# A decoder layer on one core: two chunks of the next expert's first product moved ahead of the turning of activations, and a weight ring of 16 slots

## The reference

```python
logits = (xf @ w_router + b_router)            # 32 experts, top 4 of them
top_v, top_i = lax.top_k(logits, TOP_K)
gates = jax.nn.softmax(top_v, axis=-1)
...
h = xb @ w1[e] + b1[e]                         # w1: 1024 x 2048 for each expert
x_glu = jnp.minimum(h[:, 0::2], SWIGLU_LIMIT)
x_lin = jnp.clip(h[:, 1::2], -SWIGLU_LIMIT, SWIGLU_LIMIT)
a = x_glu * jax.nn.sigmoid(SWIGLU_ALPHA * x_glu) * (x_lin + 1.0)
y = a @ w2[e] + b2[e]                          # w2: 1024 x 1024
return y.astype(F32) * gate[:, None]
```

## Time and profile before

| | |
|---|---|
| median of three runs | 1804.74 us (1802.44 to 1806.01) |
| profiled execution | 1805.31 us, its span 1803.5 us |
| experts (first token turn to last second product) | 628.9 to 1766.9 us |
| PE busy | 1512.5 us, 84% of the span |
| DMA in the expert stage, as mean busy share of the 16 DMA engines | 0.87 to 0.99 by round |
| TensorE clock granted over the span | 0.88 of full |

### The profile page before, as it was taken

The page is one execution under the profiler, slowest core; times in us unless marked ns, Lnnn a source line. Parts: engine busy times, 40 slices in busy tenths (PEclk is TensorE's granted clock), DMA queues, the critical chain, the costliest instruction groups (busy, mean ns, idle before and its releaser), DMA issues.

```text
span 1803.5 us, 33945 instructions
## 1 busy us (share of the span) xinstructions
PE 1512.5 (84%) x13484; PEld 733.8 (41%) x13484; DVE 432.2 (24%) x1005; ACT 217.2 (12%) x521; POOL 343.7 (19%) x344
## 2 busy tenths in 40 slices
PE   5999977777764599889989989989889989998991
PEld 4775565565431233433324323333333333342330
DVE  1020057332324431221212113112212212122125
ACT  1010020122101010111101011111111111011110
POOL 6120022000012312112112212212132131211212
PEclk9999975555877599999999989999989999999996
DMA  8443110200003479999998998998998999999993
GB/s 252 83 73 93 61 51 6 71 0 1 24 12 120 164 259 374 406 399 339 405 409 305 398 409 313 403 401 302 411 396 309 405 400 343 400 405 371 336 371 108
DMA packets 127719, 468.45 MB, mean 260 GB/s; under 512 B 31862, under 2 KB 52442, under 8 KB 94768
## 3 DMA queue, kind: packets, MB, share of 16 engines
q1 hardware_dynamic: 99088, 425.46, 59.6%
q0 software_dynamic: 27728, 37.99, 9.4%
q10 hardware_dynamic: 736, 2.65, 0.4%
HBM read 443.54 MB, written 23.42 MB: 259 GB/s over the span
## 4 chain that ended last, share of the span: by engine, by line
PE 53%; DVE 9%; issue 3%; DMA 1%; ACT 0%; POOL 0%; SPq 0%; DVEq 0%; POOLq 0%; ACTq 0%
PE PS L1156 32%; PE PS L1179 19%; DVE mix L1598 2%; DVE qmT L1603 2%; DVE qmT L1605 2%; PE PS L1169 1%; DVE qmT L1602 1%; DVE qmT L1599 1%; PE PS L1133 1%; DVE smalls L1646 0%; DVE ring L1656 0%; DVE ring L1658 0%; DMA smalls<-token_lists 0%; DMA expert_rows<-mix,smalls 0%; DMA ring<-expert_rows 0%
## 5 line engine op out<-in xcount | busy, mean ns | idle before, releaser
L1156 PE MATMUL PS<-ring,mix 128*32 128x512 f32 x5632 | 631.5, 603 | 38.5 <-issue 37.1
L1156 PEld LDWEIGHTS PS<-ring,mix 128*32 128x32 f32 x5632 | 190.7, 112 | 461.2 <-issue 449.3
L1179 PE MATMUL PS<-ring,mix 128*32 128x256 f32 x5632 | 345.6, 406 | 0.0
L673 POOL DMA_INDIRECT expert_rows<-mix,smalls x88 | 139.0, 1579 | 886.4 <-issue 657.7
L1179 PEld LDWEIGHTS PS<-ring,mix 128*32 128x32 f32 x5632 | 187.1, 117 | 141.9 <-issue 40.9
L1598 DVE TENSOR_TENSOR mix<-PS,kn 128x512 f32<-128x512 f32 x88 | 60.9, 692 | 564.1 <-PE PS L1156 556.0
L817 ACT ACTIVATE qmT<-qmT 128x256 f32<-128x256 f32 x88 | 36.6, 416 | 665.5 <-DVE qmT L1599 665.5
L911 PE MATMUL PS<-xT,ring 128*128 128x48 f32 (+1 forms) x384 | 104.0, 434 | 0.0
L664 POOL DMA_INDIRECT mix<-x_rows,smalls x94 | 92.8, 988 | 43.4 <-issue 33.4
L1169 PE MATMUL PS<-cst,qmT 128*128 128x128 f32 x176 | 39.5, 308 | 68.5 <-DVE qmT L1605 67.7
L897 PE MATMUL PS<-ring,xT 128*128 128x256 f32 (+1 forms) x400 | 89.7, 386 | 0.6 <-DVE xT L1251 0.6
(11 more groups left out here) (361 smaller groups left out, 968.5 us busy)
## 6 DMA issues: line engine op xcount, KB each, us to landing
ring<-in_w_moe_dram SPq DMA_DIRECT2D x384, 1024.0 KB, 14.5
ring<-in_w_in_dram SPq DMA_DIRECT2D x9, 1024.0 KB, 16.3
ring<-in_w_out_dram SPq DMA_DIRECT2D x4, 1024.0 KB
expert_rows<-X ACTq DMA_DIRECT2D x5, 512.0 KB
X<-in_x_prompt_dram SPq DMA_DIRECT2D x4, 512.0 KB, 5.5
ring<-in_state_mlstm_C_dram POOLq DMA_DIRECT2D x1, 2048.0 KB, 14.8
ring<-in_w_in_dram SPq DMA_DIRECT2D x8, 256.0 KB, 9.8
out_dram<-ring POOLq DMA_DIRECT2D x1, 2048.0 KB, 10.8
```

Source lines behind the costliest of these rows:

```text
L673: nc.gpsimd.indirect_dma_start(out=y_blocks, out_offset=bass.IndirectOffsetOnAxis(ap=lists[a][:, g, 1:2].bitcast(U32), axis=0), in_=ysb[g] ...
L1156: ins = mm(bank(g)[32 * t:32 * t + 32, :], xgT[XBUF[a][g]][:, P * (k % 2) + 32 * (k // 2):P * (k % 2) + 32 * (k // 2) + 32], ring[:, SLOT[ ...
L1179: ins = mm(bank(g)[32 * t:32 * t + 32, 0:256], aT[g % 2][:, P * (f % 2) + 32 * (f // 2):P * (f % 2) + 32 * (f // 2) + 32], rowpair(s)[:, f ...
```

## The change

- **Ring.** Slots 12 and 13 lie over the dead `xT` buffer, 14 and 15 over the dead `X` buffer. Loads go round the 16 slots in the order in which PE uses the chunks; item s waits for item s-16 (`slot_freed`). Bias and lists are loaded after w1's last chunk, a list three experts ahead.
- **PE.** Expert n's chunks 0 and 1 of w1 are multiplied between the first product and the turning of activations of expert n-1. What is left of the first product (chunks 2 to 7) has the turning of the next expert's tokens after chunk 4 instead of after chunk 7. Odd experts accumulate in banks 4 and 5, and activations turn through banks 6 and 7.
- **Loops.** The last round is written out after a loop of seven rounds on every engine. The gathers for experts 32 and 33, whose rows nobody used, are gone.
- Smaller: the router's scratch moves out of `xT`; seven semaphores of the decode attention become two.

```diff
-AHEAD = E + 2
+AHEAD = E
+BANK0 = (0, 4, 0, 4)
+TURN = 4
+EARLY = 2
-SLOT = [3, 4, 5, 0, 1, 2, 6, 7, 8, 9, 10, 11]
+SLOT = [3, 4, 5, 0, 1, 2, 6, 7, 12, 13, 8, 9, 10, 11, 14, 15]
+SLOTS = len(SLOT)
...
+def stream_w1(n, k):
+    return 12 * n + (k - 4 if k < EARLY else k) if n else k
+def stream_w2(n, c):
+    return 12 * n + 8 + EARLY + c
...
+            def slot_freed(j, s):
+                t = s - SLOTS
...
+                b, u = (t - 8) // 12, (t - 8) % 12
+                if u == EARLY + 3:
+                    sp.wait_ge(l2_mm, first_group(j, b + 1))
+                elif u == 11:
+                    sp.wait_ge(l1_mm, first_group(j, b + 2))
+                elif u < EARLY + 3:
+                    sp.wait_ge(chunk_used, j * (10 * ROUND) + (10 * b + 8 + u))
+                else:
+                    sp.wait_ge(chunk_used, j * (10 * ROUND) + (10 * b + 7 + u))
...
+            def expert_loads(j, a):
...
+                    for k in range(EARLY):
+                        s = 12 * a + 8 + k
+                        slot_freed(j, s)
+                        load_chunk(after, k, SLOT[s % SLOTS])
+                for c in range(4):
+                    s = stream_w2(a, c)
...
+                    slot_freed(j, s)
+                    load_chunk(e, 8 + c, SLOT[s % SLOTS])
...
+                for k in range(EARLY, 8):
+                    s = 12 * (a + 1) + k
+                    if isinstance(n, int) and n == 0 and s == 14:
+                        sp.wait_ge(y_set, 16 * (NT + 2))
+                    slot_freed(j, s)
+                    load_chunk(after, k, SLOT[s % SLOTS])
...
+                sp.wait_ge(b1_shuf, n + 1)
+                load_bias(after)
+                if not (isinstance(n, int) and n + 3 >= E):
+                    sp.wait_ge(y_done, first_group(j, a) + 2)
+                    load_list(expert_at(n + 3), (a + 3) % ROUND, a + 3)
...
+            def expert_rows(j, a):
+                n = j * ROUND + a
+                for g in range(GROUPS[a]):
+                    if g == GROUPS[a] - 1 and not (isinstance(n, int) and n + 2 >= E):
+                        gather(n + 2, first_pair(j, a + 1), (a + 2) % ROUND)
+                    scatter(first_group(j, a), a, g, [scattered_before(j, a, b) for b in range(4)])
...
             def expert(j, a):
                 group = first_group(j, a)
+                if not (isinstance(j, int) and j * ROUND + a == E - 1):
+                    turned_tokens(first_pair(j, a + 1), (a + 1) % ROUND)
                 sigmoid(group, 0)
-                turned_tokens(first_pair(j, a + 1), (a + 1) % ROUND)
...
             def expert(j, a):
-                n, group = j * ROUND + a, first_group(j, a)
-                nxt = (a + 1) % ROUND
-                before = GROUPS[a - 1]
-                first_product(n, a, first_pair(j, a + 1), [group + (3 - before + min(g, before - 1)) for g in range(GROUPS[a])])
-                turn_tokens(n + 1, nxt, [gathered(j, a + 1, g) for g in range(GROUPS[nxt])])
+                n, group, nxt = j * ROUND + a, first_group(j, a), (a + 1) % ROUND
+                last = isinstance(n, int) and n == E - 1
+                for k in range(EARLY, KT):
+                    s = 12 * a + k
+                    first_product(a, k, SLOT[s % SLOTS], landed(j, s))
+                    if k == TURN and not last:
+                        turn_tokens(n + 1, nxt, [gathered(j, a + 1, g) for g in range(GROUPS[nxt])])
+                if not last:
+                    pe.wait_ge(xt_ready, first_pair(j, a + 2))
+                    pe.wait_ge(y_done, group + 2)
+                    for k in range(EARLY):
+                        s = 12 * a + 8 + k
+                        first_product(nxt, k, SLOT[s % SLOTS], landed(j, s))
                 turn_activations(group, 0)
...
-            with pe.Fori(0, ROUNDS) as j:
+            pe.wait_ge(xt_ready, 2)
+            for k in range(EARLY):
+                first_product(0, k, SLOT[k], landed(0, k))
+            with pe.Fori(0, ROUNDS - 1) as j:
                 for a in range(ROUND):
                     expert(j, a)
+            for a in range(ROUND):
+                expert(ROUNDS - 1, a)
```

More of the change, by code:

```diff
@@ L112 @@
 N_STREAM = len(CHUNKS) + 4
-BEFORE = [sum(stream_incs(t) for t in range(s, N_STREAM, STREAM)) if s < STREAM else 0 for s in range(RING)]
+BEFORE = [sum(stream_incs(t) for t in range(s, N_STREAM, STREAM)) if s < STREAM else 0 for s in range(SLOTS)]
 def chunk_units(c):
@@ L155, in scattered_before, with loads_of @@
     return j * (16 * YUSE[g]) + 16 * (PRIME + use)
+def stream_w1(n, k):
+    return 12 * n + (k - 4 if k < EARLY else k) if n else k
+def stream_w2(n, c):
+    return 12 * n + 8 + EARLY + c
+def loads_of(i):
+    return sum(s % SLOTS == i and s not in [stream_w1(E, k) for k in range(EARLY)] for s in range(stream_w2(E - 1, 3) + 1))
 class Chain:
@@ L477, in _ @@
             load_list(expert_at(1), 1, 1)
[L479 to L486, removed]
-                    sp.sem_inc(steps, 1)
[L488 to L500, removed]
@@ L505, in _ @@
+            for a in range(ROUND):
+                expert_loads(0, a)
+            with sp.Fori(1, ROUNDS - 1) as j:
                 for a in range(ROUND):
-                    n = j * ROUND + a
-                    expert_loads(n, expert_at(n), first_group(j, a), (j, a))
+                    expert_loads(j, a)
+            for a in range(ROUND):
+                expert_loads(ROUNDS - 1, a)
             sp.wait_ge(extra_ready, 1)
@@ L848, in _ @@
             act.dma_start(y_dram[NTOK:NTOK + P, :], X[:, 0, :]).then_inc(y_set, 16)
-            with act.Fori(0, ROUNDS) as j:
+            with act.Fori(0, ROUNDS - 1) as j:
                 for a in range(ROUND):
                     expert(j, a)
+            for a in range(ROUND):
+                expert(ROUNDS - 1, a)
             n_over = act.value_load(n_extra, min_val=0, max_val=OVER)
@@ L1608, in expert @@
                 n, group, ahead = j * ROUND + a, first_group(j, a), (a + 2) % ROUND
-                read_list(ahead, a, j * 128 + 64 * (1 + (a + 2) // 2),
-                          [scattered_before(j, a - 1, g) for g in range(GROUPS[ahead])])
+                if not (isinstance(n, int) and n + 2 >= E):
+                    read_list(ahead, a, j * 128 + 64 * (1 + (a + 2) // 2),
+                              [scattered_before(j, a - 1, g) for g in range(GROUPS[ahead])])
                 spread_bias(n)
                 for g in range(GROUPS[a]):
-                    activations(group, g)
+                    activations(group, a, g)
             link.loop([(dve_chain, 3 * PER), (idx_ready, 4), (b1_shuf, 4), (g_ready, PER), (a_ready, PER)])
-            with dve.Fori(0, ROUNDS) as j:
+            with dve.Fori(0, ROUNDS - 1) as j:
                 link.start_round(j)
@@ L1621, in _ @@
                 dve.sem_inc(steps, 1)
-            link.end_loop(ROUNDS)
+            link.end_loop(ROUNDS - 1)
+            for a in range(ROUND):
+                expert(ROUNDS - 1, a)
             link.loop([(dve_chain, 12), (idx_ready, 1), (b1_shuf, 1), (g_ready, 4), (a_ready, 4)])
```

183 lines of the change are left out of this document (105 added, 78 removed).

## The result

| | before | after |
|---|---|---|
| median of four runs each | 1805.38 us (1802.44 to 1810.23) | 1854.22 us (1853.35 to 1855.06) |
| profiled execution, span | 1805.31, 1803.5 us | 1855.06, 1853.2 us |
| granted clock over the span | 0.88 | 0.87 |
| experts (first token turn to last second product) | 628.9 to 1766.9 us, 142 a round | 631.4 to 1817.2 us, 148 a round |
| ratio | | 1.0252 (1.0234 to 1.0271) |

The forecast was 1793.5 us in a range of 1762 to 1818. The result lies 60.7 us above the forecast and 36 above the upper end of its range.

What follows compares the result with a forecast made beforehand. PE, not DMA, was taken to bound the expert stage. Terms -104 + 69 + 26 + 6 - 6.7 - 1.4 = -11 us took the profiled 1805.3 to 1794, adjusted to the median as 1793.5 us; range 1762 to 1818.

Steps and rivals of the forecast that it cites:

- (1): PE's idle time before the turning of activations goes for 31 of 32 experts: 65 us saved.
- (2): Second products and a = 3's first product, slowed by low clock behind the activation gap, get 39 us back.
- (3): Earlier turning of tokens: PE waits for gathers, net 3.6, 1.1 and 4.5 us for a = 1, 2, 3; +69.
- (4): First products behind the token waits: lower clock costs 1.7 us 15 times, nothing after 1.1 us waits; +26.
- (5): Group 0's activation copy on ScalarE, once hidden in the gap, now delays PE: 0.2 x 31, +6 us.
- (6): Last round as straight code: one of seven jumps goes, 5.0 + 1.7, -6.7 us.
- (7): At the end, POOL's last scatter starts earlier without two unused gathers ahead of it: -1.4 us.
- (8): Ring of 16 and order of loads: 0 us, since no wait on a slot is there to shorten.
- B: Chance 0.2: fuller ring makes gathers land later, each us costing one at 23 token turns; 1.5 us gives 1828.
- A: Chance 0.15: token waits do not show and DMA bounds the round at 132 us, giving 1716 us.
- C: Chance 0.05: DMA already bounds the expert stage, whose 1138 us stay; 1797 to 1805 us.
- rival E: Chance 0.03: low clock of second products is not from the short gaps and stays; 39 us more, 1832.

## Why the prediction was wrong

The clearest account is by place. The time from the end of the third chunk to the start of the fourth, less the same in the kernel with early gathers (0.7, 0.5 and 1.0 us), is the net wait. What the first-product row behind it takes beyond the same row in the kernel with early gathers (10.51, 2.78 and 1.92 us) is the clock. Both are summed over all rounds of the trace:

| us | a = 1 | a = 2 | a = 3 | in all |
|---|---|---|---|---|
| net wait, forecast | 3.6 | 1.1 | 4.5 | 69 |
| net wait, measured, mean | 5.7 | 2.4 | 7.3 | 116 |
| clock behind it, forecast | 1.7 | 0 | 1.7 | 26 |
| clock behind it, measured, mean | 2.1 | 1.2 | 1.4 | 36 |
| times | 8 | 8 | 7 | |

Measured this makes 152 us where the prediction had 95. The 57 us of difference are nearly the whole miss of 60.7.

(1) **The activation gap** went as worked out: 3.5 us of 67.7 are left, where 2.7 were forecast. Right.

(2) **Its clock** came back in the second products: 28 us of the 33. Only the last expert, which has no successor and keeps its gap, is still slow there. The 6 us that the term also claimed for a = 3's first product (9.5 over all rounds, 1.8 of them idle pieces that the prediction's "The trace has no wait inside a first product" passes over) were not the gap's: the granted clock over that row, 1169.57 to 1184.40, was 1.00 in the trace of before, and the run with early gathers in the old kernel gets them back with 68.3 us of gaps in place. That part was put down to the wrong cause, and the changed kernel got it back all the same.

(3) **The token waits** are the step that failed, and in it one number: the landing, read from the last issue "plus 6.5, or 6.7". The places, the count, PE's arrival and the time of issue were right. The landing time came from a trace in which w2's 4 KB packets were in flight at that point, and the change alters the order of the loads. I had the two facts in hand, the change's order of slots and the size of a row of w1 and of w2, and costed "ring of 16, order of loads" at 0 because no wait for a slot was there to shorten. Under the old order the same turning costs 87 to 90 us for the forecast 95; under the new one, 152. For a = 3, 9.5 us from issue (1052.57) to the turning that waited for it (1062.03) stand against 6.7.

(4) **The clock behind the waits** fell as forecast behind the long ones. The value of 0 for a = 2 was wrong, since the wait there had become 2.4 us in the mean and the clock fell behind it as well in six rounds of eight: 10 us of the miss. This followed from (3).

(5) ScalarE's copy: 7.8 us for a forecast 6. (6) Six jumps, 28.5 us; the seven before were 35.3 of the 37.1 in the earlier trace rows. Right. (7) At the end POOL's last scatter starts 0.8 us behind the last weighting. Right. (8) No wait for a chunk: right as to waits. DMA's share of 0.95 is the forecast's. As to the order of loads it was wrong, as said.

By the terms as measured, the gap -64, the second products -28, a = 3's first product -9.5, the token waits +116, their clock +36, ScalarE's copy +8, the jump -7 and the end -1.4 make +50, against +49.8 between the two profiled executions.

**The rivals.** B was the right one in its place and its price (every us of delay costs one at 23 turns, slower from 0.7 us), but its reason and its size were not. It spoke of a fuller ring with no lull, and priced 1.5 us of delay. The delay is 2.3 us in the median, and DMA near E was full before as well. A ring that is just as full lands gathers in 6.1 to 7.6 us beside 4 KB packets (tokens turned after chunk 7). B's own estimate for 2.3 us, 1793.5 + 23 x 2.3 = 1846, lacks only the clock that the longer waits cost. "7.1 was the longest" was no bound: the trace of before records the landing of only 24 of its 86 gathers, none of them of the two-group experts whose wait for a = 2 was forecast, and nearly all beside w2's packets. A (the floor at 132 us a round) did not come with this change, but one edited line more reaches it. C is refuted by 400 GB/s held over whole rounds. The rule of the Trainium skill on idle gaps (TensorE: Matmul & The Clock Gate, section "Why this matters for your kernels"), on which rival E stood, was right that the new waits cost clock, and the second products' 7.11 us show that the short gaps had cost it too.

**Shown and not shown.** Shown is that the landing follows the size of the weights' packets: across kernels (8.8, 6.9 and 6.2 us for 8, 4 and 2 KB in the same order of loads, 6.5 with the old order) and inside two kernels that load each chunk at once (9.6 against 6.9, and 9.0 against 6.7). The wait for tokens falls with it. How the DMA engines share themselves between the two queues was not measured. The Trainium skill, DMA: Bandwidth & Descriptors, section "Queues, rings and completion order", says that a DMA engine takes its queues in turn, a packet at a time. A gather of many small rows would by that stand behind one of the weights' packets at each turn, and longer behind larger ones. The landing times agree in direction. The page gives no size for it and its packet is a bundle of descriptors, which need not be what the profile counts as one, so the way in which it happens is argued and not shown.

## What to carry to other kernels

A latency read from a trace belongs to the traffic it ran in: if the change also reorders other transfers, look up what will be in flight at that moment, by size of packet, before reusing the number. Work moved ahead on one engine needs its inputs moved ahead too: here it was enough to issue the gathers in front of the scatters that POOL would wait for, an edit of one line that turned +2.5% into -3.4%. And where a forecast stands on a margin of about a microsecond repeated 23 times, bound that microsecond from outside the trace's own conditions.

## What the runs showed of the hardware

- Indirect gathers landed in 6.5 us (median) beside packets of 4 KB and in 8.8 beside packets of 8 KB, with DMA at 376 to 401 GB/s. Inside one kernel three took 9.6 to 10.0 us beside 415 packets of 8 KB, and four took 6.1 to 7.6 beside 61.
- The price of small packets: whole stretches ran at 400 GB/s with w1's 8 KB rows, 392 with 4 KB and 351 with 2 KB, at shares of 1.01 to 1.04. The number of loads rose with it, one, two and four a chunk, so the two are not told apart.
- Loads of w1 to 64 partitions instead of 128, with w2's still to 128, brought 234 GB/s at a share of 0.97.
- The clock fell to 0.63 granted behind idle pieces of 1.86 and 0.75 us with a transposing of 0.41 us between them, as it had to 0.56 behind 0.72 and 1.95 us in the kernel before. A wait can also be free: in the old kernel with the early turning, PE stood 4.1 to 4.4 us between third and fourth chunk for a = 1 in every round, and the 80 matmuls behind took 10.5 to 11.3 us in four rounds and 8.79, full clock, in the four others.
